# Two levels of a head in one visit of PE

## The reference

```python
u = rms_norm(h, norm1_gain[l])
proj = u @ w_in[l]
hq, hf, hi, hg, aq, ak, av = jnp.split(proj, SPLITS, axis=-1)
o_rec = hgrn2_mixer(hq, hf, hi, hg, lb_all[l], hgrn_out_gain[l])
o_att = swa_sink_mixer(aq, ak, av, q_norm_gain[l], k_norm_gain[l], attn_sinks[l])
h = h + jnp.concatenate([o_rec, o_att], axis=-1) @ w_out[l]
u = rms_norm(h, norm2_gain[l])
h = h + (jax.nn.silu(u @ w_ffn_gate[l]) * (u @ w_ffn_up[l])) @ w_ffn_down[l]

# inside hgrn2_mixer, for each chunk, with f the forget gate, k = 1 - f, b = cumsum(log f)
decay = exp(b[t] - b[s]) for s <= t
scores = einsum('bhtc,bhsc,bhtsc->bhts', q, k, decay)
o_intra = einsum('bhts,bhsv->bhtv', scores, v)
o_inter = einsum('bhtc,bhcv->bhtv', q * exp(b), state)
o = rms_norm(o_intra + o_inter, out_gain) * silu(g)
```

## Time and profile before

| what | before |
| --- | --- |
| median of three runs | 1108.48 us (1107.81 to 1108.62) |
| the profiled execution itself | 1109.35 us |
| its span, first to last instruction | 1107.3 us |
| granted clock of TensorE, mean | 0.998 |
| VectorE, ScalarE, GpSimd busy | 675.4, 510.7, 361.9 us |

### The profile page before, as it was taken

The page is one execution under the profiler, slowest core; times in us unless marked ns, Lnnn a source line. Parts: engine busy times, 40 slices in busy tenths (PEclk is TensorE's granted clock), DMA queues, the critical chain, the costliest instruction groups (busy, mean ns, idle before and its releaser), DMA issues.

```text
span 1107.3 us, 16217 instructions
## 1 busy us (share of the span) xinstructions
PE 1086.6 (98%) x6338; PEld 884.6 (80%) x6338; DVE 675.4 (61%) x869; ACT 510.7 (46%) x822; POOL 361.9 (33%) x314
## 2 busy tenths in 40 slices
PE   8999999999999999999999999999999999999998
PEld 7998766778878787777888888888888878888876
DVE  6305598588698958885333343334233587777776
ACT  7413456657566635554333333333333454545531
POOL 0201222200000003107445536454544743534362
PEclk9999999999999999999999999999999999999999
DMA  8101100111106123112133313322331785445433
GB/s 279 45 1 41 55 20 5 35 40 39 40 1 210 30 90 131 77 58 104 57 124 108 136 43 127 121 91 91 124 124 58 248 319 155 153 148 166 129 100 152
DMA packets 37243, 112.74 MB, mean 102 GB/s; under 512 B 4912, under 2 KB 9776, under 8 KB 35760
## 3 DMA queue, kind: packets, MB, share of 16 engines
q1 hardware_dynamic: 37168, 111.71, 29.6%
HBM read 83.12 MB, written 28.57 MB: 101 GB/s over the span
## 4 chain that ended last, share of the span: by engine, by line
PE 90%; DVE 6%; issue 2%; ACT 1%; DMA 1%; POOL 0%; SPq 0%; DVEq 0%; POOLq 0%; ACTq 0%
PE ps L1330 28%; PE ps L1332 27%; PE ps L1331 27%; PE ps L1543 1%; PE ps L1516 1%; PE ps L1347 1%; PE ps L1558 1%; PE ps L1560 1%; DMA x<-xT 1%; PE ps L1563 1%; PE ps L1500 1%; PE ps L1569 1%; DVE sc L1842 0%; DVE yacc L2084 0%; DVE smax L1846 0%
## 5 line engine op out<-in xcount | busy, mean ns | idle before, releaser
L1702 DVE TENSOR_TENSOR glo<-graw,ghi 128x1024 fp32r<-128x1024 f32 x21 | 26.2, 1247 | 148.2 <-POOL s34raw L691 147.3
L1330 PE MATMUL ps<-uhi,whi 128*128 128x512 f32 x272 | 112.4, 413 | 0.0
L1332 PE MATMUL ps<-uhi,wlo 128*128 128x512 f32 x272 | 106.3, 391 | 0.0
L1331 PE MATMUL ps<-ulo,whi 128*128 128x512 f32 x272 | 106.3, 391 | 0.0
L2084 DVE TENSOR_TENSOR yacc<-ps,yacc 128x512 f32<-128x512 f32 x104 | 68.8, 683 | 9.1 <-PE ps L1332 9.0
L1330 PE MATMUL ps<-ubhi,arhi 128*128 128x512 f32 x176 | 68.9, 392 | 2.4 <-DVE yacc L2084 2.3
L1330 PE MATMUL ps<-ohi,s12hi 128*128 128x512 f32 x168 | 66.1, 393 | 3.3 <-DVE s12lo L1708 1.8
L1331 PE MATMUL ps<-ublo,arhi 128*128 128x512 f32 x176 | 68.5, 389 | 0.0
L1332 PE MATMUL ps<-ubhi,arlo 128*128 128x512 f32 x176 | 68.5, 389 | 0.0
L1330 PE MATMUL ps<-ohi,s34hi 128*128 128x512 f32 x168 | 65.4, 390 | 0.8 <-ACT ps L1173 0.8
L1332 PE MATMUL ps<-ohi,s12lo 128*128 128x512 f32 x168 | 66.1, 393 | 0.0
(11 more groups left out here) (337 smaller groups left out, 2950.6 us busy)
## 6 DMA issues: line engine op xcount, KB each, us to landing
hidden<-hst SPq DMA_DIRECT2D x11, 1792.0 KB, 6.0
ubraw<-hidden SPq DMA_DIRECT2D x33, 512.0 KB, 5.5
graw<-wg SPq DMA_DIRECT2D x21, 512.0 KB, 4.5
uraw<-wu SPq DMA_DIRECT2D x21, 512.0 KB, 3.6
wraw<-wproj SPq DMA_DIRECT2D x17, 512.0 KB, 3.5
araw<-wd SPq DMA_DIRECT2D x22, 384.0 KB, 4.8
h<-xT SPq DMA_DIRECT2D x8, 512.0 KB, 4.8
h_kept<-h SPq DMA_DIRECT2D x16, 256.0 KB, 2.0
```

What stands on the lines that cost most here:

```text
L1330: nc.tensor.matmul(out, whi_, xhi_, start=first, stop=False, skip_group_check=seeded)
L1331: nc.tensor.matmul(out, whi_, xlo_, start=False, stop=False, skip_group_check=seeded)
L1332: return nc.tensor.matmul(out, wlo_, xhi_, start=False, stop=last, skip_group_check=seeded)
L1702: nc.vector.tensor_tensor((glo2 if g == 2 else glo[g % 2])[:, :], graw[g % 2][:, :], ghi[g % 2][:, :].bitcast(F32), ALU.subtract).then_inc ...
```

## The change

The list is dealt out differently; no instruction is added, removed or changed, and lines below the edit move down by one.

```diff
--- before.py
+++ after.py
@@ -139,18 +139,19 @@
     order += mix(take(8 + H0_EXTRA), steps)
     for h in range(NH):
         last = h == NH - 1
-        steps = []
-        for lv in range(LEVELS):
-
-            steps.append([("LM", h, lv)])
-            steps[lv] += [("LX", h, lv + 2)] if lv + 2 < LEVELS else []
-            steps[lv] += [("LV", h, lv + 4)] if lv + 4 < LEVELS else []
-        steps[0] = [("LX", h, 1), ("LV", h, 3)] + steps[0] + [("HI", h)]
+        steps = [[] for _ in range(LEVELS)]
+        steps[0] = [("LX", h, 1), ("LV", h, 3)]
+        for lv in range(0, LEVELS, 2):
+            steps[lv + 1] += [("LM", h, lv), ("LM", h, lv + 1)]
+            for k in (lv + 2, lv + 3):
+                steps[lv + 1] += [("LX", h, k)] if k < LEVELS else []
+                steps[lv + 1] += [("LV", h, k + 2)] if k + 2 < LEVELS else []
+        steps[0] += [("HI", h)]
         if h:
             steps[0] += [("OM", h - 1)]
-            steps[1] = [("ON", h - 1)] + steps[1]
+            steps[1] += [("ON", h - 1)]
             steps[2] += [("OX", h - 1, 0)]
-            steps[3] += [("OX", h - 1, 1)]
+            steps[3] = [("OX", h - 1, 1)] + steps[3]
         if last:
             steps[5] += [("MS", 6), ("ML", 6)]
             order += mix(take(n_p + 32 - taken[0]), steps)
```

## The result

| | before | changed |
| --- | --- | --- |
| median of the five runs of each | 1108.62 us (1107.81 to 1111.93) | 1113.59 us (1111.05 to 1114.34) |
| ratio | | 1.0034, 95% interval 1.0020 to 1.0048 |
| profiled execution, its span | 1109.35, 1107.3 us | 1111.05, 1109.0 us |

The change makes the kernel slower by 0.34%, or 3.8 us, 2.2 to 5.3 us by the interval; 3.0 us more, 1111.5, was predicted. Added to the 1108.48 us that the prediction started from, the ratio gives 1112.2 us. The median of the changed kernel itself, 1113.59 us, is 5.0 us above the median of before and lies above 1113.0, where the stated range ended. The changed kernel's profiled execution is its fastest run, and its span is only 1.7 us longer. The two profiles differ elsewhere too, so I laid them side by side dense matmul by dense matmul.

A forecast was written before the change was run, and what follows sets the result against it. PE was taken to bound the kernel, busy 1086.6 us, 98% of the span. Heads 0 to 3 at +0.1, +0.6, +2.8 and -0.5 sum to +3.0 us on the median 1108.48: 1111.5 us, range 1109.0 to 1113.0.

The forecast's parts named there:

- The switches: PE, all four heads: fewer visits, at 0.20 us for entry and exit together, save 2.07 us.
- Head 0: The 0.60 us saved turn into waits inside the second and third visit; +0.1 us.
- the doubled copy: VectorE: of two copies in direct succession the second lasts 0.45 us and not 0.33, 0.12 us more.
- Head 1: VectorE idles 2.8 us ahead of OX 0 for ON, so PE waits for LM 4 and LM 5; +0.6 us.
- Head 2: VectorE idles for PE, then for ON; ML 1 is late and O 0 0 waits 3.0 us; +2.8 us.
- Head 3: More dense matmuls between visits, so PE doesn't wait and the saving stays; -0.5 us.
- The sum: Over the four heads, +3.0 us, for a time of 1111.5 us.
- The cause: ON behind LV 5 on ScalarE makes VectorE idle 2.8 us ahead of OX 0, so ML 1 is late for PE.
- The third rival: Head 2: weight unit's load 1.6 us later delays the spreads, PE waits 1.2 us; +4.2 us in all, chance 0.10.
- The first two rivals: First: all waits covered, -2.07 us, chance 0.05. Second: VectorE doesn't stand behind ON, -1.1 us, chance 0.10.

The follow-up runs named there:

- head 2 alone: The kernel before with the change in head 2 only; 1112.15 us, ratio 1.0029.
- ON first: The changed kernel with ON put back to the front of steps[1], nothing else; 1110.60 us, ratio 1.0005.
- ON late alone: The kernel before with only ON moved behind LM 1, LX 3 and LV 5; 1108.56 us, ratio 0.9995.
- OX 0 behind the products: The changed kernel with OX 0 and OX 1 moved behind the products of level 5, ON still behind LV 5; one run, 1113.59 us.
- mixed: The kernel before with all three pairs in heads 1 and 3, levels 2/3 and 4/5 paired in head 2, none in head 0; 1111.37 us, ratio 1.0020.
- mixed without the pair of levels 4 and 5: The kernel before with all pairs in heads 1 and 3, only levels 2 and 3 paired in head 2; 1107.14 us, ratio 0.9986.

## Why the prediction was right

- **The switches**, -2.07 us: the direction and the 0.20 us of a visit held. The term was too small: heads 3 and 1 without waits win 0.9 to 1.0 us and not 0.49, since the second level and OM alone take some 0.1 us less each. Over heads 1 to 3 that is about 1.4 us more. In heads 0 to 2 of the changed kernel it didn't show, since waits decided there.
- **Head 0**, +0.1 predicted, +0.33 by the shifts. The savings turned into waits for `M` of 1.30 and 0.50 us. The term that was too small is the doubled copy, priced at 0.12 us more than two single ones. It takes 0.88 us (237.49 - 236.61) where two single ones take 0.66, so 0.22 us each and not 0.12:

```profile
236.61 0.99 DVE L1944 COPY_PREDICATED near<-smask,ps 128x256 f32<-128x256 int8 x2
237.49 0.68 DVE L1936 TENSOR_TENSOR M<-K,D 128x512 f32<-128x512 f32 x1
```

- **Head 1**, +0.6 predicted, +0.54. 2.8 us of idle time ahead of OX 0 predicted, 2.71 measured; waits of PE for LM 4 and LM 5 as said, with OM's 0.1 us and a pair's on the other side.
- **Head 2**, +2.8 predicted, +2.61. The wait for ML 1 was to be 3.0 us and is 3.11; the idle times ahead of it, 2.0 and 2.8, are 1.80 and 2.71.
- **Head 3**, -0.5 predicted, -0.93.
- **The sum**, +3.0 predicted, +2.55 by the shifts and +2.2 to +5.3 by the runs. The heads of the profiled execution, the changed kernel's fastest, explain the lower part of that interval. The clock explains part of the rest. The longer executions of one kernel are those with the lower mean clock (table in the last section), and the changed kernel's five have 0.998 to 0.996. Set beside the executions of before with the same mean clock, which come from a later series, they take 2.2 to 4.8 us more, 3.1 in the mean, where the means of the two kernels' five lie 3.9 us apart. So about 0.8 us go with the lower clock. Whether it fell behind the wait for ML 1 in them isn't shown; in head 2 alone it did, 0.9 us more. It is a cost of a wait that the prediction left out.
- **The cause** was right with one limit, which the prediction didn't see: ON behind LV 5 is free while the copy of level 2 and the products of level 4 stand ahead of OX 0. It takes both, the pair and ON's place, to get the 3.1 us; with one of them alone the wait for `mlo` is 0.8 us (ON first) or none (ON late alone). And OX 0 is not the only step that stands behind ON: the unit's low part does too, by way of the high part, as OX 0 behind the products showed.
- **The third rival** was real but covered: in the changed kernel the load landed 1.1 us later than before (345.94), the spreads ended at 350.03, and PE came at 351.00. They cost 1.7 us with ON first and 3.3 us in the mixed kernel, where PE comes early. The first two rivals fell: waits weren't covered, and VectorE did stand behind ON. That VectorE works its queue in order, which the prediction took from the Trainium skill, page "TensorE: Matmul & The Clock Gate", section "Architectural detail: the array is 16× 32×32, not 1× 128×128", is what the rows after show: in head 1 LM 2 and LM 3 are through by 285.77, and no copy of them runs before OX 0 does at 287.57.

## What to carry to other kernels

Merging visits of PE is worth their entry and exit, here 0.2 to 0.3 us each, only while the engines in between have slack; read the slack first, as the time between the last producer's end and the consumer's start, and pair only where it is larger than what the pair moves. When steps of a list are regrouped, look at every step that rides along: here ON behind LV 5 made 2.3 of the 3.1 us of waiting, and a weight unit's high part ahead of the spreads cost 1.7 and 3.3 us. And when one wait is taken away, look for the one that it covered.

## What the runs showed of the hardware

- Two groups of small matmuls back to back, in different PSUM banks, take 0.1 us less together than apart (1.27 to 1.29 us against 1.38; once 1.40), beside the entry and exit.
- Two copies in direct succession, the second on the same tile as the first, take 0.88 us on VectorE (0.93 behind a wait, 326.94 to 327.87), where two single ones take 0.66.
- A wait of PE has a second price that its length doesn't show. Behind waits of 3.1 us (head 2 alone), 3.3 us (mixed) and 4.2 us (OX 0 behind) the granted clock was 0.81, 0.57 and 0.53 in the next whole window of 5 us, with matmuls 0.42 us apart in place of 0.23. By the shifts that was 0.9, 2.6 and 1.8 us more than the wait. Behind a wait of 3.1 us in the changed kernel it stayed at 1.00. The same holds at another place: all ten profiles have a wait of 1.80 to 1.82 us for `s12lo` between 505 and 514 us, and behind it the clock fell in six of them, before among them, and stayed at 1.00 in four, the changed kernel among them. What decides it is open.
- Executions of one kernel with a lower mean granted clock mostly take longer. Mean time in us, number of executions in brackets:

| kernel | 1.000 | 0.999 | 0.998 | 0.997 | 0.996 | 0.995 |
| --- | --- | --- | --- | --- | --- | --- |
| before | 1107.08 (3) | 1106.88 (2) | 1108.83 (20) | 1110.84 (5) | 1111.19 (5) | |
| changed | | | 1112.35 (2) | 1113.41 (2) | 1114.34 (1) | |
| head 2 alone | 1109.42 (1) | | 1111.76 (3) | 1112.60 (6) | 1112.83 (1) | 1114.84 (1) |
| mixed | | | 1109.75 (4) | 1112.01 (2) | 1110.74 (2) | 1113.07 (4) |

- ScalarE waited for the load of the weight unit in head 2 in all ten kernels, until 342.36 us (mixed without the pair of levels 4 and 5) to 345.94 us (changed). Only what stands behind it was changed here; no run issued the load earlier.
